# The opening of a decoder-trunk step: page rows loaded by kind, one kind ahead, eight of the transfers issued by ScalarE

## The reference

```python
def compress(rows, pos, w1, b1, w2):
    B, T = rows.shape[:2]
    c = rows.reshape(B, T // CMP_STRIDE, CMP_STRIDE, NSA_KV, HEAD_DIM)
    blocks = jnp.concatenate([c[:, :-1], c[:, 1:]], axis=2) + pos[None, None, :, None, :]
    n_cmp = blocks.shape[1]
    flat = blocks.transpose(0, 1, 3, 2, 4).reshape(B, n_cmp, NSA_KV, CMP_LEN * HEAD_DIM)
    return jax.nn.gelu(flat @ w1 + b1) @ w2

kc = compress(rows[:, :, 0], pos[0], w1[0], b1[0], w2[0])
vc = compress(rows[:, :, 1], pos[1], w1[1], b1[1], w2[1])
```

## Time and profile before

| | |
|---|---|
| median of 3 runs | 1929.6 us (1925.34 to 1931.41) |
| the profiled execution | 1930.48 us, its span 1928.8 us |
| PE busy | 1806.5 us, 94% of the span |
| DVE, ACT, POOL busy | 988.4, 735.2, 504.1 us |
| DMA, whole span | 229.31 MB, mean 119 GB/s |
| stretch 0 to 20 us | PE busy 0.10 us, DMA 178 GB/s |
| stretch 20 to 40 us | PE busy 13.94 us, DMA 211 GB/s |

### The profile page before, as it was taken

One profiled execution on the slowest core, in us unless ns is written; L12 is line 12 of the kernel. 1 busy time (PEld: TensorE's weight loads), 2 busy tenths in 40 slices (PEclk: granted clock), 3 DMA queues, 4 the chain that ended last, 5 costly groups with the idle time before them and its releaser, 6 DMA issues. The chain is left out here.

```text
span 1928.8 us, 31267 instructions
## 1 busy us (share of the span) xinstructions
PE 1806.5 (94%) x11465; PEld 1593.3 (83%) x11465; DVE 988.4 (51%) x1909; ACT 735.2 (38%) x1477; POOL 504.1 (26%) x604
## 2 busy tenths in 40 slices
PE   4998999999888799999997998999999999999996
PEld 4888787998644588889886878999999999876784
DVE  4233421242334688888887442333333333465997
ACT  3234411211322288888886331111111111233353
POOL 5020022420535252222213010112222111133523
PEclk9899999999999899999998998999999999999999
DMA  8544343346969893333311221111111111254543
GB/s 190 79 110 147 123 157 121 115 139 227 330 218 317 179 250 80 67 77 82 84 67 66 80 70 51 44 43 43 44 54 43 54 43 55 74 201 152 197 137 145
DMA packets 169904, 229.31 MB, mean 119 GB/s; under 512 B 45018, under 2 KB 113477, under 8 KB 169665
## 3 DMA queue, kind: packets, MB, share of 16 engines
q1 hardware_dynamic: 143298, 152.77, 26.5%
q0 software_dynamic: 24400, 72.81, 13.3%
q10 hardware_dynamic: 2080, 2.10, 0.4%
HBM read 192.65 MB, written 40.24 MB: 121 GB/s over the span
## 5 line engine op out<-in xcount | busy, mean ns | idle before, releaser
L121 PE MATMUL gate_acc<-o_T_hi,w_gate_split_hi 128*128 128x352 f32 x528 | 171.3, 324 | 2.3 <-ACTq L2828 2.3
L121 PE MATMUL up_acc<-o_T_hi,w_up_split_hi 128*128 128x352 f32 x528 | 171.3, 324 | 0.7 <-DVEq L2892 0.7
L122 PE MATMUL gate_acc<-o_T_lo,w_gate_split_hi 128*128 128x352 f32 x528 | 170.0, 322 | 0.0
L122 PE MATMUL up_acc<-o_T_lo,w_up_split_hi 128*128 128x352 f32 x528 | 169.9, 322 | 0.0
L123 PE MATMUL gate_acc<-o_T_hi,w_gate_split_lo 128*128 128x352 f32 x528 | 169.8, 322 | 0.0
L123 PE MATMUL up_acc<-o_T_hi,w_up_split_lo 128*128 128x352 f32 x528 | 169.8, 322 | 0.0
L2404 DVE TENSOR_TENSOR pa_probs_T_lo<-pa_t,pa_probs_T_hi 128x512 fp32r<-128x512 f32 (+3 forms) x264 | 139.8, 549 | 19.9 <-ACT pa_probs_T_hi L2331 17.9
L2316 ACT ACTIVATE pa_scores<-pa_scores,pa_neg_max 128x640 f32<-128x640 f32 (+3 forms) x192 | 143.5, 747 | 14.0 <-DVE pa_neg_max L2356 10.5
L2950 POOL TENSOR_TENSOR w_gate_split_lo<-w_gate,w_gate_split_hi 128x1024 fp32r<-128x1024 f32 x21 | 50.4, 2399 | 340.5 <-ACT w_gate_split_hi L2838 340.5
L2331 ACT ACTIVATE pa_probs_T_hi<-pa_t 128x512 fp32r<-128x512 f32 (+3 forms) x264 | 122.9, 485 | 38.4 <-PE pa_t L2255 36.8
L121 PE MATMUL y_acc<-w_down_split_hi,act_split_hi 128*128 128x512 f32 x308 | 123.9, 402 | 7.6 <-DVE act_split_lo L3256 3.2
(11 more groups left out here) (456 smaller groups left out, 4750.0 us busy)
## 6 DMA issues: line engine op xcount, KB each, us to landing
w_down_raw<-in_w_down SPq DMA_DIRECT2D x59, 512.0 KB, 4.7
fox_k_pages<-in_cache_fox_kv SPq DMA_DIRECT2D x64, 256.0 KB, 5.3
w_rows<-in_cache_fox_kv POOLq DMA_DIRECT2D x48, 256.0 KB, 4.7
w_gate<-in_w_gu SPq DMA_DIRECT2D x22, 512.0 KB, 3.9
w_up<-in_w_gu SPq DMA_DIRECT2D x22, 512.0 KB, 4.0
w_rows<-in_w_in SPq DMA_DIRECT2D x5, 2048.0 KB, 9.4
sel_pages<-in_cache_nsa_kv POOLq DMA_DIRECT2D x64, 128.0 KB, 5.4
pa_k_fox<-scratch_kf_d POOLq DMA_DIRECT2D x32, 256.0 KB, 6.9
```

The source lines that it names most:

```text
L121: pe.matmul(out, a[0][at], b[0][bt], start=start, stop=False)
L122: pe.matmul(out, a[0][at], b[1][bt], start=False, stop=False)
```

## The change

The rows of sequences 0 and 1 are loaded by kind. `load_kind` issues transfers of 32 KB (64 partitions, 2 runs of 64 numbers) where `load_rows` issued 64 KB (4 runs), so these two sequences take 64 transfers and not 32. All of kind 0 is asked for ahead of kind 1: SP takes four pages of sequence 0 and two of sequence 1, POOL the same numbers, ACT the other four pages of sequence 1 (eight transfers). Quarters 1, 2 and 3 of `w1` are issued by ACT, each behind other work of ACT; SP issues none. Of the four turns of kind 1, `products(0)` now holds two (behind slices 9 and 13) and `products(1)` two (behind slices 1 and 5), and ACT and DVE take all turns of the first batch before they round quarters 2 and 3.

```diff
@@ during
             if m < 0:
                 during[-1] += mine
+            elif m == 0:
+                during[0] += mine[:2]
+                during[1] += mine[2:]
@@ new helper
+        def load_kind(eng, which, k, q, p0, p1):
+            at = q * PAGES
+            _, pages = nc.values_load_multi_w_load_instructions(
+                c.pt[0:1, at + p0:at + p1], engines=[which], min_val=0, max_val=d["cache_nsa_kv"].shape[1] - 1)
+            for p in range(p0, p1):
+                side = slice((p % 2) * 64, (p % 2) * 64 + 64)
+                src = d["cache_nsa_kv"][0, ds(pages[p - p0], 1)].rearrange("a (n r) w g e -> (a n) r (w g) e", r=2)
+                for r in range(2):
+                    eng.dma_start(rows[q][side, p // 2, 2 * k:2 * k + 2, r, :], src[:, r, 2 * k:2 * k + 2, :]).then_inc(s_kind[k][q][which == mybir.EngineType.Pool], 16)
@@ SP
-            for q in range(seqs(0)):
-                load_rows(sp, mybir.EngineType.SP, q, 0)
-            load_w1(sp, 2)
-            load_w1(sp, 3)
+            load_kind(sp, mybir.EngineType.SP, 0, 0, 0, 4)
+            load_kind(sp, mybir.EngineType.SP, 0, 1, 0, 2)
+            for q in range(2):
+                load_kind(sp, mybir.EngineType.SP, 1, q, 0, 4)
             load_rows(sp, mybir.EngineType.SP, 2, 0)
             sp.dma_start(pos[:, :], ...)
@@ POOL
-            for q in range(3):
-                load_rows(pool, mybir.EngineType.Pool, q, 1)
+            load_kind(pool, mybir.EngineType.Pool, 0, 0, 4, 8)
+            load_kind(pool, mybir.EngineType.Pool, 0, 1, 4, 6)
+            for q in range(2):
+                load_kind(pool, mybir.EngineType.Pool, 1, q, 4, 8)
+            load_rows(pool, mybir.EngineType.Pool, 2, 1)
@@ PE
-                    if j % 4 == 1 and between:
+                    if j % 4 == 1 and between and (m or j > 8):
                         turn(between.pop(0))
@@ ACT
             load_w1(act, 0)
-            load_w1(act, 1)
+            for p in (2, 6):
+                load_kind(act, mybir.EngineType.Activation, 0, 1, p, p + 2)
             act.wait_ge(s_pad, 6)
             round_w1(0)
+            act.wait_ge(s_kind[0][0][0], 128)
+            load_w1(act, 1)
+            for t in during[-1]:
+                round_rows(t)
+            load_w1(act, 2)
             round_w1(1)
-            for t in during[-1] + during[0]:
+            for t in during[0]:
+                round_rows(t)
+            load_w1(act, 3)
+            for t in during[1]:
                 round_rows(t)
             round_w1(2)
             round_w1(3)
@@ DVE
             rest_w1(0)
+            for t in during[-1]:
+                rest_rows(t)
             rest_w1(1)
-            for t in during[-1] + during[0]:
+            for t in during[0] + during[1]:
                 rest_rows(t)
             rest_w1(2)
             rest_w1(3)
```

More of the change, by code:

```diff
@@ L195, in front @@
         s_rows = [[ph.sem(f"cmp_{part}_pages_loaded{i}") for i in range(SB)] for part in ("first", "last")]
+        s_kind = [[[ph.sem(f"cmp_kind{k}_{who}_pages_loaded{q}") for who in ("queue", "pool")] for q in range(2)] for k in range(2)]
         s_raw = [ph.sem(f"cmp_w1_loaded{i}") for i in range(2)]
@@ L330, in turn @@
                 q = first_seq[b] + s
-                if k == 0 and half == 0:
-                    pe.wait_ge(s_rows[0][q % SB], 128 * (q // SB + 1))
-                    pe.wait_ge(s_rows[1][q % SB], 128 * (q // SB + 1))
+                if b == 0 and half == 0:
+                    pe.wait_ge(s_kind[k][q][0], 192 if (k, q) == (0, 1) else 128)
+                    pe.wait_ge(s_kind[k][q][1], 64 if (k, q) == (0, 1) else 128)
+                if b and k == 0 and half == 0:
+                    loads = q // SB + (q % SB == 2)
+                    pe.wait_ge(s_rows[0][q % SB], 128 * loads)
+                    pe.wait_ge(s_rows[1][q % SB], 128 * loads)
                 if n >= 2:
@@ L508, in _ @@
             act.activation(pos_s[:, :, :, 0], ps_s[:, 0:32].rearrange("p (k j) -> p k j", k=2), ACT.Copy).then_inc(s_ph, 1)
-            for t in during[1]:
-                round_rows(t)
             gelu(0)
@@ L560, in _ @@
             dve.tensor_tensor(pos_s[:, :, :, 1], ps_s[:, 0:32].rearrange("p (k j) -> p k j", k=2), pos_s[:, :, :, 0], ALU.subtract).then_inc(s_ps, 1)
-            for t in during[1]:
-                rest_rows(t)
             dve.wait_ge(s_pp, 1)
```

## The result

| | before | after |
|---|---|---|
| median, compared on one chip | 1925.34 us (1921.37 to 1931.41, 5 runs) | 1942.28 us (1937.39 to 1943.85, 5 runs) |
| span of the profiled execution | 1928.8 us | 1942.2 us |
| mean granted clock of TensorE | 0.975 | 0.971 |

The ratio is 1.0076, with a 95% interval of 1.0057 to 1.0095: 14.6 us more (11.0 to 18.3). The two spans differ by 13.4 us. I had forecast slower, by + 11.1 with a range of + 9 to + 13. The change measured lies above that range, though its interval reaches into it. The time of 1942.28 lies inside the range of 1938 to 1944 partly by luck, since the kernel before was 4.3 us faster in this comparison than the 1929.6 that I started from.

A forecast was written before the change was run, and what follows sets the result against it. SP's queue was taken to bound the kernel from 44.08 to 113.57, PE having 3.74 us of slack. 1930.48 + 11.1 = 1941.6 for the profiled execution, so a median of 1941.0; range 1938 to 1944, 8 in 10 within 1932 to 1947.

The forecast's parts named there:

- The request of the position rows: SP's queue in the opening: position rows asked for at 39.0 and not 35.03, behind more issues.
- the rival of cheaper small issues: SP's queue: a 32 KB issue costs 0.332 us, not 0.598; + 2.0 to + 3.7, 1933 us; chance 0.12.
- SP and ACT did not hold each other up: Rival, opening: SP and ACT issues block each other, SP loses up to 4.8 us; + 15.9, 1946.4 us; chance 0.10.
- Its landing: Position rows' transfer in the opening: lands 3.3 us after its request, at 42.3.
- The first product: PE's opening: first product starts at about 24 and not 29.87, gaining nothing at the end.
- The path from there to the roundings: PE and ACT, products(1): from landing at 42.3 through both turns at the lower clock, roundings start at 48.7, not 37.60.
- the distance between the two turns: PE in products(1): second turn 2.85 us after the first, at the lower pace.
- From the roundings to `s_wd` 4: ACT and DVE: 6.45 us from roundings to end of splits, so s_wd 4 at 55.15, 11.1 later.
- Which of two paths sets the end: From s_wd 4 to the rows of sequence 5: SP's queue, not PE, sets the end; + 11.1 us.
- SP's chain at + 11.1: SP's queue from 44.08 on, tables, store, copies, rows of sequence 5: moves whole, 11.1 us later.
- POOL: POOL's own queue: four issues more (12 x 0.6 us), with no wait there that PE needs before 55.
- The rival of a faster block: Opening moves forward as one block by the first product's 5.9 us: 1924.6 us; chance 0.09.

The follow-up runs named there:

- the last run: Changed kernel with all later edits, POOL's half of sequence 2 held back, and misc and misc_s asked for behind rows of sequences 5 to 7 and copies: ratio 0.996.

## Why the prediction was right

*The request of the position rows*, forecast at 39.0, came at 39.79. A transfer of 32 KB costs SP what one of 64 KB costs, which I had only argued, and 36 issues with their address steps and page reads fill the queue from 5.79 to 39.75. One line's operations in the changed kernel, ns minimum, median, maximum:

```profile
L254 SPq DMA_DIRECT2D cmp_rows<-in_cache_nsa_kv x28: 598/598/745, 5.8 to 31.5; - x28
...
L254 ACTq DMA_DIRECT2D cmp_rows<-in_cache_nsa_kv x8: 606/621/731, 5.9 to 12.5; - x8
```

That settles the rival of cheaper small issues (0.332 nowhere). SP and ACT did not hold each other up where it mattered: SP kept its median of 598, and ACT's eight took 606 to 731 ns. All eight of ACT's issues and eight of SP's fall between 5.79 and 13.1 us, and together they last 9.6 us or more, so they overlapped. Of the exclusive lock that the Trainium skill states ("Perfetto Trace Analysis", "DMA Instruction — HWDGE (DVE, Sync)") the trace shows nothing on SP. The Trainium skill's rule that sequencer time is usually small beside the transfer ("DMA: Bandwidth & Descriptors", "Issuing engines are not separate DMA queues") does not carry over to this queue: 36 issues set the time of the 37th, and asking for it first was worth about 13 us.

*Its landing* was the first size that was off: 4.9 us and not 3.3, 44.7 and not 42.3.

```profile
cmp_pos_sb<-in_cmp_pos SPq DMA_DIRECT2D x1, 16.0 KB, 4.9
```

ACT's quarter 3 had been asked for at 34.27 and landed at 40.2, and rows asked for by POOL and SP were in flight; no run tells these apart. Together with 0.8 at the request it is 2.4 us. The first product at 26.08 and not 24 looks of the same kind: rows of sequence 1 were in flight beside quarter 1, asked for at 15.27. It cost nothing, as the standstill covered it.

*The path from there to the roundings*: forecast 6.4 us at the lower clock (42.3 to 48.7), measured 7.1 (44.74 to 51.85). The granted clock was 0.50 there until about 51, as forecast:

```profile
44.00:48.00 4.00, 3.26 (x15) 0.50 0.51 74
```

The term that was too small is the distance between the two turns: 3.41 us (46.43 to 49.84) for the 2.85 that I took from 31.29 to 34.14 in the kernel before. That stretch was not all at the lower pace. Its products start every 0.21 us up to 33.4 and every 0.12 from there on. Two products of each kind, and the granted clock of 28 to 32 us (1.00, behind the count in brackets; 32 to 36 us reads the same):

```profile
30.22 0.41 PE L363 MATMUL cmp_hid<-cmp_rows_T_lo,cmp_w_split_hi 128*128 128x256 f32 x1
30.43 0.41 PE L364 MATMUL cmp_hid<-cmp_rows_T_hi,cmp_w_split_lo 128*128 128x256 f32 x1
...
34.82 0.28 PE L364 MATMUL cmp_hid<-cmp_rows_T_hi,cmp_w_split_lo 128*128 128x256 f32 x1
34.94 0.29 PE L362 MATMUL cmp_hid<-cmp_rows_T_hi,cmp_w_split_hi 128*128 128x256 f32 x1
...
28.00:32.00 4.00, 2.13 (x11) 1.00 1.08 275
```

So there was a slower pace, but the granted clock does not record it, and what slows those first products no run shows. In the changed kernel, at 0.50, products start every 0.21 us from one turn to the other.

From the roundings to `s_wd` 4 it was 6.45 again. So `s_wd` 4 came 14.25 late and not 11.1: 0.8 at the request, 1.6 at the landing and 0.7 for the slower path.

*Which of two paths sets the end.* I had SP's chain at + 11.1 and PE at + 9.9 with 3.74 of slack, so that SP's decided. The size of both was too low by three, and they moved nearly together (SP's copies + 14.5, PE's `positions` + 13.1), so that waits for rows of much the same length remained (3.3 us for 3.74). This step is at most half right, and that the sum came out near is partly luck. The run with sequence 5 ahead of the store shows that without SP's part 10.6 us of the loss stay, where my sum would have left 6.2, 9.9 less 3.74. And in the two runs with SP's store 3.9 and 5.1 us late (64.66 and 65.81), PE waited for no rows at all. What the traces show is that PE's lateness at `positions` sets the end, and that the slack it can use up is the wait together with what the clock does on the way, which I had not looked at although has 60 to 64 us at 0.50 with PE busy throughout.

*POOL*: I wrote of four issues more and reckoned with twelve; twelve is right (36 for 24).

*The rival of a faster block* needed the position rows by 29.8. The run that asks for them at the head of the queue shows that this was not enough: the split of quarter 3 was next, then the rows beside that quarter, and then the store. Only with each of these moved did an earlier opening reach the end, and then as 2.5 us at `positions`, not as the 5.9 of the rival.

## What to carry to other kernels

A small transfer that one late instruction needs costs what stands ahead of it in its queue: count the issues ahead of it, not its bytes, and put it first. The slack of a wait can be more than its length, as the granted clock was 0.50 for 5 us behind this one: a delay of 8.5 us in the opening cost 2.2 at the next phase. It does not follow that taking the wait away gives back as much. Here it gave back the idle time alone, so look at the granted clock of the whole stretch, not only at the row of the wait. And when a wait is taken away, name the next one in line before the run: here four stood in a row (position rows, split of quarter 3, rows of sequence 1, rows of sequences 5 and 6), and no kernel that kept one of them or made it anew won more than 3.3 us.

## What the runs showed of the hardware that I had not expected

- With a request of 1 MB on ACT's queue at 28.85, small transfers issued at 28 to 32 us took about twice as long to land on SP's and POOL's queues: 6.9 and 6.7 us with it, 3.4 and 3.0 in the changed kernel (4.2 and 3.9 in the run with the position rows first), and 4.9 on SP when POOL's were held back. Beside quarter 2, at 24 to 28 us in the changed kernel, it was 4.8 and 5.4.
- While the replicated store (1532 KB) is in flight, little moves, with or without `misc_s` beside it. The stretch of the kernel before, its last two numbers DMA share and GB/s:

```profile
80.00:84.00 4.00, 4.00 (x32) 1.00 0.46 48
```

  In one run, rows asked for in it, from 91.36 on, were what PE waited for until 114.24. SP's issue itself can take long: SP's request of `misc` right behind the store in the kernel before, and behind the copies in the last run, were:

```profile
61.61 10.12 SPq L276 DMA_DIRECT2D misc<-in_c_misc  x1
```

```profile
123.13 0.59 SPq L296 DMA_DIRECT2D misc<-in_c_misc  x1
```

- Two executions of the same opening differ by up to 0.9 us in when the rows of sequence 1 land: PE's turn behind them starts at 25.46 in the kernel before and at 26.36 in the run with the position rows later, with the same queues up to there. In the two kernels before with rows put ahead of the copies it starts at 26.09 and 26.26, and `positions` comes 1.2 and 1.5 us late, with nothing changed ahead of it. So a difference of that size in `positions` alone tells nothing of an edit.
